# The final norm of a two-layer decoder: sum of squares by halves, weight before the root, scaling spread over three engines

## The reference

```python
def rms_norm(x, w):
    y = x * lax.rsqrt(jnp.mean(x * x, axis=-1, keepdims=True) + NORM_EPS)
    return y * w
...
        h = h + 0.5 * swiglu_ffn(rms_norm(h, ffn2_norm[layer]), ffn2_w_gate_up[layer], ffn2_w_down[layer])
    return rms_norm(h, final_norm)
```

## Time and profile before

| | us |
|---|---|
| median of 3 runs | 1110.52 |
| lowest, highest | 1110.36, 1112.6 |
| the profiled execution | 1110.62 |
| its span | 1108.6 |
| PE busy in the span | 1067.3 (96%) |
| DVE busy | 610.6 (55%) |
| ACT busy | 529.7 (48%) |
| POOL busy | 106.1 (10%) |

### The profile page before, as it was taken

The page is one execution under the profiler, slowest core; times in us unless marked ns, Lnnn a source line. Parts: engine busy times, 40 slices in busy tenths (PEclk is TensorE's granted clock), DMA queues, the critical chain, the costliest instruction groups (busy, mean ns, idle before and its releaser), DMA issues.

```text
span 1108.6 us, 14578 instructions
## 1 busy us (share of the span) xinstructions
PE 1067.3 (96%) x5480; PEld 900.1 (81%) x5480; DVE 610.6 (55%) x823; ACT 529.7 (48%) x772; POOL 106.1 (10%) x117
## 2 busy tenths in 40 slices
PE   6999999987999999999999998999998999999997
PEld 4888888865788888888888887989997988888885
DVE  5555554568565456446454645583596455545542
ACT  6535343455564354336443435582476346344431
POOL 0000000142000000000000004540333100000000
PEclk9999999999999999999999999998998999999999
DMA  8665565431345645645646553420341065465520
GB/s 302 193 201 179 191 226 188 147 131 39 111 157 189 210 168 199 218 152 170 209 154 224 189 191 118 153 77 1 113 152 41 3 226 170 156 215 191 217 93 38
DMA packets 123310, 174.68 MB, mean 158 GB/s; under 512 B 7152, under 2 KB 97536, under 8 KB 123264
## 3 DMA queue, kind: packets, MB, share of 16 engines
q1 hardware_dynamic: 120832, 172.01, 45.6%
q10 hardware_dynamic: 2432, 2.03, 0.6%
HBM read 172.98 MB, written 1.05 MB: 157 GB/s over the span
## 4 chain that ended last, share of the span: by engine, by line
PE 87%; DVE 7%; ACT 3%; POOL 1%; issue 1%; DMA 1%; ACTq 0%; SPq 0%; DVEq 0%; POOLq 0%
PE bank L1302 25%; PE bank L1304 25%; PE bank L1303 25%; PE bank L1593 4%; PE bank L1370 2%; PE bank L1564 1%; PE bank L1587 1%; DVE w_lo L924 1%; PE bank L1678 1%; PE bank L1330 1%; DVE prob L1098 1%; DVE X L1221 1%; ACT y_sb L624 1%; DMA w_raw<-in_ffn_w_gate_up 1%; ACT w_hi L621 0%
## 5 line engine op out<-in xcount | busy, mean ns | idle before, releaser
L924 DVE TENSOR_TENSOR w_lo<-w_raw,w_hi 128x2048 fp32r<-128x2048 f32 x153 | 365.1, 2391 | 153.7 <-ACT w_hi L621 153.4
L621 ACT ACTIVATE w_hi<-w_raw 128x2048 fp32r<-128x2048 f32 x161 | 307.8, 1919 | 116.0 <-PE bank L1304 115.5
L1302 PE MATMUL bank<-w_hi,xT_hi 128*128 128x512 f32 x784 | 313.3, 400 | 6.6 <-DVE xT_lo L944 5.3
L1304 PE MATMUL bank<-w_hi,xT_lo 128*128 128x512 f32 x784 | 306.7, 391 | 0.0
L1303 PE MATMUL bank<-w_lo,xT_hi 128*128 128x512 f32 x784 | 306.1, 390 | 0.0
L1302 PEld LDWEIGHTS bank<-w_hi,xT_hi 128*128 128x128 f32 x784 | 147.7, 188 | 38.8 <-DVE xT_lo L944 5.9
L1304 PEld LDWEIGHTS bank<-w_hi,xT_lo 128*128 128x128 f32 x784 | 147.6, 188 | 31.7
L1303 PEld LDWEIGHTS bank<-w_lo,xT_hi 128*128 128x128 f32 x784 | 147.9, 189 | 29.9 <-issue 0.7
L655 ACT ACTIVATE silu_g<-bank,rstd 128x256 f32<-128x256 f32 x88 | 37.0, 471 | 250.1 <-PE bank L1304 250.1
L1302 PE MATMUL bank<-w_hi,hT_hi 128*128 128x512 f32 x352 | 138.1, 392 | 0.0
L1304 PE MATMUL bank<-w_hi,hT_lo 128*128 128x512 f32 x352 | 137.1, 390 | 0.0
(11 more groups left out here) (265 smaller groups left out, 1094.7 us busy)
## 6 DMA issues: line engine op xcount, KB each, us to landing
w_raw<-in_ffn_w_gate_up SPq DMA_DIRECT2D x176, 512.0 KB, 4.7
w_raw<-in_ffn_w_down SPq DMA_DIRECT2D x88, 512.0 KB, 4.0
w_raw<-in_gdn_w_in SPq DMA_DIRECT2D x32, 512.0 KB, 4.5
w_raw<-in_attn_w_in SPq DMA_DIRECT2D x12, 512.0 KB, 4.3
w_raw<-in_attn_w_out SPq DMA_DIRECT2D x8, 512.0 KB, 4.3
w_raw<-in_gdn_w_out SPq DMA_DIRECT2D x8, 512.0 KB, 5.5
x_sb<-in_x SPq DMA_DIRECT2D x2, 512.0 KB, 5.1
out<-y_sb SPq DMA_DIRECT2D x4, 256.0 KB, 2.1
```

Of the source, the lines that this page charges most:

```text
L621: act.activation(w_hi[u0 % RING][:], w_raw[u0 % RING][:], ACT.Copy).then_inc(hi_ready, 1)
L924: dve.tensor_tensor(w_lo[u0 % RING][:], w_raw[u0 % RING][:], w_hi[u0 % RING][:].bitcast(F32), ALU.subtract).then_inc(split_ready, 1)
L1302: pe.matmul(out_ap, a[0], b[0], start=start, stop=False, **kw)
L1304: return pe.matmul(out_ap, a[1], b[0], start=False, stop=stop, **kw)
```

## The change

All of it lies behind PE's last unit. DVE no longer forms y in one step behind the root. It multiplies each quarter of x_sb by the weight as soon as the quarter's residual is written (TENSOR_TENSOR into `y_sb`), and the root is multiplied in afterwards: ACT scales quarters (0,0) and (1,0) by a Copy with a scale, POOL scales (0,1) and DVE (1,1) by a TENSOR_SCALAR. ACT squares each half by itself into a scratch tile (`silu_g`) with its own sum; DVE turns the first half's sum into a partial mean and adds the second's. `y_ready` becomes four semaphores, `xw_ready` is new. The store of (1,0) is issued from ACT's queue, the other three from SP's. Two small tiles are added and a spacer is shortened by as much, so that no other tile moves.

```diff
-        sb("to_grid_1", [P, 72])
+        ssq_half = sb("ssq_half", [P, TT, 2])
+        mean_half = sb("mean_half", [P, TT])
+        sb("to_grid_1", [P, 66])
...
-        y_ready = sem("y_ready")
+        xw_ready = sem("xw_ready")
+        y_ready = [[sem(f"y_ready{t}_{half}") for half in range(2)] for t in range(TT)]
@@ SP @@
-                    sp.wait_ge(y_ready, 2 * t + half + 1)
-                    sp.dma_start(out[0, t * P:(t + 1) * P, at], y_sb[:, t, at]).then_inc(out_stored, 16)
+                    if (t, half) != (1, 0):
+                        sp.wait_ge(y_ready[t][half], 1)
+                        sp.dma_start(out[0, t * P:(t + 1) * P, at], y_sb[:, t, at]).then_inc(out_stored, 16)
@@ POOL @@
+            pool.wait_ge(rstd_ready, RSTD_FINAL + 1)
+            pool.wait_ge(xw_ready, 2)
+            pool.tensor_scalar(y_sb[:, 0, BANK:D], y_sb[:, 0, BANK:D], rstd[:, 0:1], None,
+                               ALU.mult).then_inc(y_ready[0][1], 1)
@@ ACT @@
-            for t in range(TT):
-                act.wait_ge(resid_ready, 4 * 5 + 2 * t + 2)
-                square(6, t, x_sb[:, t, :], y_sb[:, t, :])
-                root(RSTD_FINAL + t + 1, slice(t, t + 1))
+            def final_square(t, half):
+                act.wait_ge(resid_ready, 4 * 5 + 2 * t + half + 1)
+                act.activation(silu_g[half][:].rearrange("p t n -> p (t n)"), x_sb[:, t, half * BANK:(half + 1) * BANK], ACT.Square,
+                               accum_out=ssq_half[:, t, half:half + 1]).then_inc(ssq_ready, 1)
+            def final_scale(t, half):
+                at = slice(half * BANK, (half + 1) * BANK)
+                act.wait_ge(rstd_ready, RSTD_FINAL + t + 1)
+                act.wait_ge(xw_ready, 2 * t + half + 1)
+                act.activation(y_sb[:, t, at], y_sb[:, t, at], ACT.Copy,
+                               scale=rstd[:, t:t + 1]).then_inc(y_ready[t][half], 1)
+            final_square(0, 0)
+            final_square(0, 1)
+            final_square(1, 0)
+            root(RSTD_FINAL + 1, slice(0, 1))
+            final_scale(0, 0)
+            final_square(1, 1)
+            root(RSTD_FINAL + 2, slice(1, 2))
+            final_scale(1, 0)
+            act.wait_ge(y_ready[1][0], 1)
+            act.dma_start(out[0, P:2 * P, 0:BANK], y_sb[:, 1, 0:BANK]).then_inc(out_stored, 16)
@@ DVE @@
-            for t in range(TT):
-                for half in range(2):
-                    residual(6, 2 * t + half, 0.5)
-                inverse_rms(TT * 6 + t + 1, slice(t, t + 1))
-                dve.wait_ge(rstd_ready, RSTD_FINAL + t + 1)
-                for half in range(2):
-                    at = slice(half * BANK, (half + 1) * BANK)
-                    dve.scalar_tensor_tensor(y_sb[:, t, at], x_sb[:, t, at], rstd[:, t:t + 1], final_w[:, at],
-                                             ALU.mult, ALU.mult).then_inc(y_ready, 1)
+            def final_residual(t, half):
+                residual(6, 2 * t + half, 0.5)
+                dve.wait_ge(resid_ready, 4 * 5 + 2 * t + half + 1)
+            def final_weight(t, half):
+                at = slice(half * BANK, (half + 1) * BANK)
+                dve.tensor_tensor(y_sb[:, t, at], x_sb[:, t, at], final_w[:, at], ALU.mult).then_inc(xw_ready, 1)
+            def final_first_mean(t):
+                dve.wait_ge(ssq_ready, TT * 6 + 2 * t + 1)
+                after(dve.tensor_scalar(mean_half[:, t:t + 1], ssq_half[:, t, 0:1], 1.0 / D, EPS, ALU.mult, ALU.add))
+            def final_mean(t):
+                dve.wait_ge(ssq_ready, TT * 6 + 2 * t + 2)
+                after(dve.scalar_tensor_tensor(mean_sq[:, t:t + 1], ssq_half[:, t, 1:2], 1.0 / D,
+                                               mean_half[:, t:t + 1], ALU.mult, ALU.add))
+                dve.reciprocal(inv_ms[:, t:t + 1], mean_sq[:, t:t + 1]).then_inc(inv_ready, 1)
+            for half in range(2):
+                final_residual(0, half)
+                final_weight(0, half)
+            final_first_mean(0)
+            final_residual(1, 0)
+            final_mean(0)
+            final_weight(1, 0)
+            final_first_mean(1)
+            final_residual(1, 1)
+            final_weight(1, 1)
+            final_mean(1)
+            dve.wait_ge(rstd_ready, RSTD_FINAL + 2)
+            dve.wait_ge(xw_ready, 2 * TT)
+            dve.tensor_scalar(y_sb[:, 1, BANK:D], y_sb[:, 1, BANK:D], rstd[:, 1:2], None,
+                              ALU.mult).then_inc(y_ready[1][1], 1)
```

## The result

The changed kernel takes 1114.74 us in the median of 8 runs (1112.99 to 1115.16), the old one 1111.03 in the median of 8 (1110.36 to 1112.6). The ratio is 1.0032, with a 95% interval of 1.0022 to 1.0041: slower by 3.7 us, where 1.7 us less was forecast.

A forecast was written before the change was run, and what follows sets the result against it. PE fills 87% of the last chain, but gains could come only from the 8.2 us DVE/ACT chain behind it. The last pair's first store leaving 1.7 us earlier turns 1110.62 into 1108.9, median 1108.8; range 1108.0 to 1110.8.

The forecast's parts named there:

- the first one: Opening claim: nothing of the change lies beside PE, so only the 8.2 us behind PE can yield a gain.
- if anything ahead of 1096 moves: Sign of being wrong: anything changes before DVE's first residual of the end, at 1096.41 us in the old profile.
- residual (1,1) starts: DVE's second residual of tile 1 starts at 1101.08 against 1102.2; most of the gain was placed here.
- DVE's product beside POOL takes: DVE's weight product (1,1) runs inside POOL's scaling and is disturbed: 0.9 us in place of 0.69.
- gain of the end: Behind PE, the last pair's first store leaves at 1103.74 in place of 1105.46, so transfers end 1.7 us earlier.
- the copy's slope: POOL's scaling priced as 0.60 plus 384 elements at its one-input copy's 1.55 ns: 1.20 us.
- the wait that it was to cause: POOL's scaling delays DVE's product (1,1), so the last mean loses 0.08 us; each further tenth of POOL costs a tenth.
- both POOL rivals: POOL slow: gain 0.3 to 1.2, chance 0.18 shared with ACT's late queue; small mean waits behind POOL: up to 1111.2, 0.10.
- The transfer: Last two 256 KB stores keep the DMA engines busy 1.35 us in one piece, as before.
- the pair goes by its first issue: The last two stores are limited by the first one's issue; the second, 0.27 later, finds the engines busy.
- the rival in which the stores don't queue: Last stores cost under 1.35 us together, so ACT's issue counts: gain 2.1 to 2.3; chance 0.17, shared with a shorter chain.
- the one of a late ACT queue: ACT's last store takes 3.3 us to land: 1109.6; chance 0.18, shared with POOL slow.

The follow-up runs named there:

- whole Squares: Changed kernel at the old addresses, each final tile's Square in one instruction instead of halves; 10.31 us from first residual to end, against 10.44 with halves.

## Why the prediction was wrong

The step that failed is the first one: "nothing of the change lies beside PE, so the question is only what follows it". Two lines of the diff do lie beside PE, the ones that add tiles ahead of hT. I took the spacer's six floats for the two tiles' six and priced the lines at nothing, without looking at the addresses, where each tile is rounded up by itself. They moved hT and oT by 64 bytes and cost 5.1 us (ratio 1.0046 with nothing else changed), and none of the rivals was of this kind. The prediction's last sentence named the sign, "if anything ahead of 1096 moves", and that is what happened.

The rest, term by term, in us behind the first residual:

| step | forecast | changed kernel |
|---|---|---|
| residual (1,1) starts | 4.67 | 4.61 |
| last mean starts | 6.23 | 6.09 |
| root of tile 1 is read | 6.85 | 6.72 |
| ACT's scaling takes | 0.72 | 0.72 |
| DVE's scaling takes | 0.45 | 0.49 |
| POOL's scaling takes | 1.20 | 1.56 |
| DVE's product beside POOL takes | 0.91 | 0.69 |
| last store is issued | 7.60 | 7.47 |
| gain of the end | 1.7 | 1.8 |

Two terms were wrong, and it was luck that they did not show in the sum. POOL was 0.36 slower than the copy's slope gave, and the wait that it was to cause did not come: by the prediction's own rule, a tenth for each tenth, it would have cost 0.44 in place of 0.08. I had taken that wait from a POOL TENSOR_TENSOR, with two inputs, and applied it to a TENSOR_SCALAR, with one. Which difference between the two cases matters is not shown. With the wait gone, both POOL rivals are out too. The transfer was right in size: the last two stores kept the engines busy for 1.00 x 1.02 + 1.20 x 0.28 = 1.36, against 1.35 before. That the pair goes by its first issue held too, by the table above. So the rival in which the stores don't queue is out, and so is the one of a late ACT queue: the end came 2.9 behind ACT's issue, where a landing of 3.3 would have put it later.

On the Trainium skill's rule, page "ScalarE: Activation LUTs", section "Rules for kernel authors", to multiply on VectorE: I had said that it gives nothing here. The scaling took 0.49 on DVE and 0.72 on ACT, as the rule has it, but with both quarters of tile 1 on DVE the last byte came only 0.04 us earlier, so for the end it gave nothing that these profiles can tell. The exclusive lock that I took from the page "SBUF — State Buffer", section "SBUF: two separate sides", of the Trainium skill agrees with the earlier trace rows but not with the changed kernel: a DVE product of two SBUF inputs ran at its 0.69 inside POOL's 1.56. The measurement decides. POOL's 1.69 with whole Squares may be a trace of such a lock: DVE's product had 0.26 us left when POOL started, and POOL took 0.13 longer.

## What to carry to other kernels

A diff that adds a small tile can move every tile behind it. Before pricing the instructions, compare the addresses of the two programs, and keep PE's stationary float32 tiles on multiples of 256 bytes, where they lost nothing here. Where a change is slower, look first at whether untouched stages kept their lengths; one timing of the old kernel with only the tiles moved tells the two apart. And a wait between two engines that a trace shows for one form of instruction is not to be carried over to another form.

## What was new about the hardware

- A stationary operand of 128x128 float32 whose address lies 32, 64 or 128 bytes behind a multiple of 256 makes PE take 0.233 us a product of 512 columns in place of 0.227, at the same granted clock; at 256 bytes there is no loss. Its reason is not shown: PE's weight loads are recorded at 0.19 us in both.
- A moving operand 64 bytes off costs 0.229 in place of 0.227.
- POOL's TENSOR_SCALAR of 128x512 takes 1.56 us with and without a DVE product of two SBUF inputs that starts inside it, and that product keeps its 0.69. Once, with such a product already running when POOL started, it took 1.69.
- The last byte of two stores of 256 KB comes 2.28 to 2.33 us behind the first of their two issues, with the second 0.23 to 0.67 behind it, from the same queue or another.
- In the DeltaNet's stage, equal instructions took 225.6 us at a granted clock of 0.96 and 0.99 and 231.9 at 0.94 and 0.96, a difference larger than the whole effect under study.
